# A Strassen-style FFN decoder trunk on one core: the fourth lead unit gets its own PSUM pair, and the products, cuts and sums around it are reordered

## The reference

```
x += 0.5 * SwiGLU_1(rms(x))                  # FFN, hidden width 2816
x += W_out [ gMLP(rms(x)) ; RG-LRU(rms(x)) ]
x += 0.5 * SwiGLU_2(rms(x))                  # FFN
x += sigmoid(rms(x) @ W_pg) * (p[i] @ W_pp)
# swiglu(x) = (silu(x @ wg) * (x @ wu)) @ wd
```

## Time and profile before

| | us |
|---|---|
| median of 3 runs | 1858.75 (1858.49 to 1860.04) |
| the profiled execution | 1858.88 |
| its span, first to last instruction | 1857.2 |
| TensorE busy | 1819.7 |
| VectorE busy | 1508.2 |
| ScalarE busy | 1063.0 |

### The profile page before, as it was taken

How to read it: one execution, slowest core, us unless ns; L and a number is a source line. 1 busy time by engine, 2 the same in 40 slices (tenths; PEclk the granted TensorE clock), 3 DMA queues, 4 the chain that set the end, 5 groups by cost and what they waited for, 6 DMA issues and landing times.

```text
span 1857.2 us, 37525 instructions
## 1 busy us (share of the span) xinstructions
PE 1819.7 (98%) x14824; PEld 1797.5 (97%) x14824; DVE 1508.2 (81%) x2319; ACT 1063.0 (57%) x1538; POOL 299.4 (16%) x380
## 2 busy tenths in 40 slices
PE   7999999999999999999999999999999999999997
PEld 6999999998999999999999999999999999999997
DVE  7989978768689889787689789777775897988775
ACT  6656656545456566565466565554544665655553
POOL 0011011340120110112110110115202101011122
PEclk9999999999999999999999999999999999999998
DMA  5657579722346666795355765794223657667941
GB/s 173 155 151 188 136 199 246 216 80 69 110 134 155 175 166 152 194 262 172 124 148 127 197 167 158 209 249 147 71 92 114 162 137 194 158 160 230 237 140 47
DMA packets 81265, 297.16 MB, mean 160 GB/s; under 512 B 9344, under 2 KB 11680, under 8 KB 79312
## 3 DMA queue, kind: packets, MB, share of 16 engines
q1 hardware_dynamic: 52592, 184.87, 30.9%
q0 software_dynamic: 28512, 110.03, 27.8%
HBM read 267.00 MB, written 25.74 MB: 158 GB/s over the span
## 4 chain that ended last, share of the span: by engine, by line
PE 89%; DVE 7%; issue 2%; ACT 1%; DMA 0%; DVEq 0%; SPq 0%; ACTq 0%
PE main L764 24%; PE main L730 19%; PE main L769 12%; PE aux L764 9%; PE main L926 9%; PE aux L769 5%; PE aux L926 4%; PE aux L1028 2%; PE main L819 2%; PE aux L730 1%; PE aux L976 1%; DVE w_lo L1690 1%; PE main L1028 1%; PE aux L1048 0%; DVE tmp L1854 0%
## 5 line engine op out<-in xcount | busy, mean ns | idle before, releaser
L764 PE MATMUL main<-part_hi,w_hi 128*128 128x260 f32 x1296 | 328.5, 284 | 8.8 <-DVE tmp L1854 5.3
L764 PE MATMUL main<-part_lo,w_hi 128*128 128x260 f32 x1296 | 326.6, 283 | 0.0
L764 PEld LDWEIGHTS main<-part_hi,w_hi 128*128 128x128 f32 x1296 | 244.5, 189 | 11.6 <-DVE tmp L1854 7.7
L764 PEld LDWEIGHTS main<-part_lo,w_hi 128*128 128x128 f32 x1296 | 244.5, 189 | 0.0
L622 POOL DMA_DIRECT2D w_lo<-weights_dram x104 | 90.3, 868 | 851.1 <-ACT w_lo L1154 842.5
L769 PE MATMUL main<-part_hi,w_lo 128*128 128x260 f32 x1296 | 213.7, 282 | 0.2 <-DMA w_lo<-weights_dram 0.2
L1166 ACT ACTIVATE w_hi<-tau 128x1024 fp32r<-128x1024 f32 x104 | 109.9, 1057 | 177.0 <-PE main L769 152.4
L730 PE MATMUL main<-part_hi,w_hi 128*128 128x260 f32 x944 | 192.6, 285 | 2.0 <-DVE tmp L1738 2.0
L730 PE MATMUL main<-part_hi,w_lo 128*128 128x260 f32 x944 | 189.8, 283 | 0.0
L730 PE MATMUL main<-part_lo,w_hi 128*128 128x260 f32 x944 | 189.5, 282 | 0.0
L764 PE MATMUL main<-sig,w_hi 128*128 128x260 f32 x1280 | 181.6, 284 | 5.7 <-issue 5.7
(11 more groups left out here) (325 smaller groups left out, 4544.1 us busy)
## 6 DMA issues: line engine op xcount, KB each, us to landing
raw<-weights_dram SPq DMA_DIRECT2D x344, 512.0 KB, 3.8
w_lo<-weights_dram POOLq DMA_DIRECT2D x104, 512.0 KB, 6.4
d_part<-tmp POOLq DMA_DIRECT2D x64, 260.0 KB, 5.3
x<-d_part POOLq DMA_DIRECT2D x16, 1040.0 KB, 14.3
x_spill<-x POOLq DMA_DIRECT2D x6, 1040.0 KB, 4.9
x<-x_spill POOLq DMA_DIRECT2D x6, 1040.0 KB, 9.8
x<-x_in_dram SPq DMA_DIRECT2D x4, 520.0 KB, 6.7
x<-tmp POOLq DMA_DIRECT2D x4, 520.0 KB, 3.2
```

The costliest lines, as they stand in the source:

```text
L764: pe.matmul(ps, hi_w[:, w], xx(k), start=(start and k == 0 and b == 0), stop=False, skip_group_check=True)
```

## The change

It does five things, in each of the four FFNs.

1. The fourth lead unit (up 1) goes to `aux[1]` instead of a main pair. It waits for `std_s` instead of `evac`, and P1(0) and P1(1) wait for older evacuations.
2. In the first chunk P2(1) moves from behind P7(0) to ahead of P6(0).
3. On DVE, `tau3`, `tau4`, `hidden_out(1)` and `hidden_lo(0)` move behind `lo12` of the first tile. On ACT `copy_p1(0)` moves ahead of `hi34`, and `h_lead(1)` behind `copy_p5(0)`.
4. The copy of the two lead tiles of h into x (`copy_lead`) becomes two DMAs with a semaphore each.
5. The raw sums of h tiles 0 and 1 move from the stage with c22(3) to the stage with c22(1), and their low part comes together with that of tiles 2 and 3.

```diff
+FOURTHS = tuple(t + 1 for t in THIRDS)
...
-SUM_ORDER = ((1, 0, 2, 3), (0, 1, 2, 3))
...
+    if tiles == tiles_of(0) and t < 2 and name != "P4" and (t, name) != (1, "P7"):
+        return ({"P1": 1, "P2": 2, "P6": 5, "P5": 6, "P7": 7}, {"P1": 3, "P2": 4, "P6": 9, "P5": 10})[t][name]
...
-            return aux[0] if g in THIRDS else main[main_slot(g)]
+            return aux[0] if g in THIRDS else aux[1] if g in FOURTHS else main[main_slot(g)]
...
-            def copy_lead(f, G):
-                pool.wait_ge(evac, G)
+            def copy_lead(f, G, k):
+                pool.wait_ge(evac, G - 2 * (LEAD - 1 - k))
...
-                pool.dma_start(x[:, XT - 2:XT, :], tmp[:, 2:4, :]).then_inc(lead_copy, 16)
+                pool.dma_start(x[:, XT - LEAD + k, :], T(2 + k)).then_inc(lead_copy[k], 16)
... TensorE: the fourth lead unit, P1, the order, the down product
-                    pe.wait_ge(evac, G + 1)
+                    pe.wait_ge(std_s, stat + 1)
                     acc(bank(G + 3), 3, XT, x_hi, x_lo).then_inc(unit, 1)
...
-                            pe.wait_ge(evac, G - 2 * (1 - t))
+                            pe.wait_ge(evac, G - 3 + t)
...
-                        if t == 1:
+                        if c and t == 1:
                             pe.wait_ge(evac, G)
...
                     P1(1)
+                    if first:
+                        P2(1)
                     P6(0)
                     P5(0)
                     P7(0)
-                    P2(1)
+                    if c:
+                        P2(1)
                     P4(0)
...
-                            pe.wait_ge(std_s, stat + 1)
+                            pe.wait_ge(evac, G)
                         down_part(0, 0, whole - 1, True)
... ScalarE
-                        if first and t == 2:
+                        if first and t == 0:
                             sums_hi(l, f, c, 0)
...
                         hi12(n, S)
+                        copy_p1(0)
                         hi34(n, S)
...
-                        h_lead(l, G - 2 * LEAD, 1)
...
                     copy_p5(0)
+                    if first:
+                        h_lead(l, G - 2 * LEAD, 1)
                     hi12(n + 2, S + 1)
... VectorE, the lead of FFN 1 and 3 (the others likewise)
                             sigma_lo(stat, 3)
-                            ahead(1, S0, S)
-                            ahead(2, S0, S)
-                            hidden_lo(0)
-                            hidden_out(1)
+                            tau1(S0, S)
+                            tau2(S0, S)
...
-                        if first and t == 2:
+                        if first and t == 0:
                             sums_raw(f, c, 0)
                             sums_raw2(f, c, 0)
...
-                        if not last and t >= pairs and k % 2:
+                        if not last and t >= pairs and k % 2 and not (first and t == 1):
                             sums_lo(l, f, c, k // 2)
                         if first and t == 2:
                             sums_lo(l, f, c, 0)
+                            sums_lo(l, f, c, 1)
...
                     if first:
                         lo12(n, S)
+                        tau_sums(0, (tau3, tau4))
+                        hidden_out(1)
                         lo34(n, S)
-                        dve.wait_ge(hhi, h)
-                        hi_, lo_ = hparts(l)
-                        dve.tensor_tensor(lo_[:, LEAD - 1, :], T(3), hi_[:, LEAD - 1, :], ALU.subtract).then_inc(hlo, 1)
+                        hidden_lo(0)
                         lo_b(n, S)
```

More of the change, by code:

```diff
@@ L136, in first_tile @@
     return TILES * (2 * l + which)
-SUM_ORDER = ((1, 0, 2, 3), (0, 1, 2, 3))
 SUM_AT = ({3: 0, 1: 1, 2: 2, 4: 3}, {1: 0, 3: 1, 2: 2, 4: 3})
 def sums_of(f, c, i):
-    return KH * (DOWN_CHUNKS * f + c) + SUM_ORDER[c].index(i) + 1
+    return KH * (DOWN_CHUNKS * f + c) + i + 1
 def sums_in(f, c):
@@ L178, in main_slot @@
     layer, k = divmod(g, GROUPS)
-    return (g + layer + (k >= G_GT + V_AFTER) + sum(g > t for t in THIRDS)) % 2
+    return (g + layer + (k >= G_GT + V_AFTER) + sum(g > t for t in THIRDS + FOURTHS)) % 2
 def trunk(nc, weights, x_in, p_in, vecs_in, ln_in, bs_in, ws_in, bd_in, sc_in, sh_in,
@@ L309, in trunk @@
         sh_lo = sem("sh_lo")
-        lead_copy = sem("lead_copy")
+        lead_copy = [sem(f"lead_copy{k}") for k in range(LEAD)]
         d_second = sem("d_second")
@@ L667, in gates @@
                         if c == 0 and t == 1:
-                            copy_lead(f, G)
+                            for k in range(LEAD):
+                                copy_lead(f, G, k)
                         if c and t == 1:
@@ L1341, in ffn @@
                         hi34(n, S)
-                    copy_p1(0)
+                    if c:
+                        copy_p1(0)
                     copy_p1(1)
@@ L1603, in sums_raw @@
                 if early:
-                    dve.wait_ge(lead_copy, 16 * (f + 1))
+                    for k in range(LEAD):
+                        dve.wait_ge(lead_copy[k], 16 * (f + 1))
                 if f:
@@ L1713, in free @@
                 pending[b] = False
-            def ahead(j, n, T_):
-                if j == 1:
-                    tau1(n, T_)
-                    tau2(n, T_)
-                    tau3(n, T_)
-                if j == 2:
-                    tau4(n, T_)
-                if j == 3:
-                    lo34(n, T_)
             def ffn(l, which, u0, g0):
@@ L1739, in gate_out, with hidden_out @@
                                               ALU.mult).then_inc(evac, 1)
-                        def hidden_out(k):
+                        def hidden_out(k, n=n, G=G, fs=fs):
                             dve.wait_ge(unit, n + 2 * k + 2)
@@ L1745, in hidden_out, with hidden_lo @@
                                               ALU.mult).then_inc(evac, 1)
-                        def hidden_lo(k):
+                        def hidden_lo(k, h=h):
                             dve.wait_ge(hhi, h + k + 1)
@@ L1769, in ffn @@
                             sigma_lo(stat, 3)
-                            tau3(S0, S)
-                            tau4(S0, S)
-                            hidden_lo(0)
                         elif which:
@@ L1824, in c11 @@
                         elif first:
-                            dve.wait_ge(hlo, h)
                             dve.wait_ge(evac, G)
@@ L1851, in c22 @@
                         if first and t < LEAD:
-                            dve.wait_ge(lead_copy, 16 * (f + 1))
+                            dve.wait_ge(hlo, h - LEAD + t + 1)
+                            dve.wait_ge(lead_copy[t], 16 * (f + 1))
                         free(2 + (S + t) % 2)
@@ L1926, in ffn @@
                     lo12(n + 2, S + 1)
+                    if first:
+                        hidden_lo(1)
                     c11_r(0)
```

## The result

| | before | after |
|---|---|---|
| median, us | 1859.09 (1858.17 to 1860.04, 6 runs) | 1866.85 (1864.7 to 1868.7, 6 runs) |
| profiled execution, us | 1858.88 | 1868.59 |
| its span, us | 1857.2 | 1866.9 |

The changed kernel is slower: ratio 1.0042, 95% interval 1.0029 to 1.0055, +7.8 us by the medians. Forecast were +4.5 us and 1863.3; the time lies inside the range, near its upper end. The profiled execution of after is one of its slower ones, so in the traces there are 9.7 us to explain.

The account below looks back on a forecast made before the run. TensorE, busy 98% of the span, was taken to bound the kernel. Leads +2.2, clock +1.2 and +1.9, sums -0.8 made +4.5 us on 1858.75, so 1863.3; range 1857 to 1867.5.

Parts of the forecast that it names:

- as forecast: The main case for the whole kernel: slower by +3 to +6 us, chance 0.50.
- rival (c): The clock falls in FFN 1 and 3 too, or longer in FFN 0: +7.5 us, 1866, chance 0.14.
- What bounds, and P7(0): TensorE bounds; P7(0) waits for `copy_u2(0)` behind `gate(2)` and its load, starting 6.1 us behind `tau4`'s end, or later.
- Cost 0: The two smaller lead-copy DMAs, issued by POOL ahead of `gate(2)`'s low load, cost nothing.
- `tau4` moved: On DVE `tau4` ends later: +0.54 us in FFN 0 and 2, 4.2 us in FFN 1 and 3.
- Stands: TensorE stands 2.5 to 4 us before P7(0) in FFN 0 and 2, 1 to 1.6 in FFN 1 and 3.
- Leads at full clock: P4(0) starts shift by -0.9, +1.9, -1.1, +1.9 us in FFN 0 to 3, restarts +0.4: sum +2.2.
- Sums: Moving the sums of h on DVE shortens the stand before P4(4): -0.2 us in each of four, -0.8.
- The clock: Low clock behind the lead stands: +1.2 us in FFN 2, +1.9 in FFN 0, 0 in FFN 1 and 3.
- The sum: All terms for the whole kernel: +4.5 us, 1863.3 us, slower by 0.24%.
- Rival (d): Faster: the sums bring all they can (-0.3 us), and where `gate(2)` does not wait for its load -7.4, 1851; chance 0.14.

Follow-up runs that it names:

- Experiment 1: The changed kernel with `copy_u2(0)` and `copy_p5(0)` ahead of `gate(2)` on ACT in the first chunk: 1859.88 us.
- experiment 4: The changed kernel with the second copy of a lead tile issued behind the low load of the third tile instead of ahead of it: 1866.69 us.
- Experiment 5: The kernel before, with only the sums of h spread (part 5 of the change): 1858.32 us.
- experiment 11: The changed kernel once more, unaltered, a single execution: 1873.84 us.
- experiment 3: The changed kernel with `tau3` and `tau4` back ahead of `lo12` of the first tile on DVE: 1856.52 us.
- experiment 8: The changed kernel with `copy_u2(0)`, `copy_p5(0)` ahead of `gate(2)`, P2(1) back between P7(0) and P4(0), `tau3`, `tau4` ahead of `lo12`: 1853.84 us.

## Why the prediction was right, and where it was too small

The waits were forecast rightly, one by one; the time came out higher, and +7.8 us lies outside the forecast's own band for "as forecast" (+3 to +6). It is nearest to rival (c), +7.5, of which one half ("or longer in FFN 0") came true in the profiled execution, with a longer stretch in FFN 2 besides.

**What bounds, and P7(0).** Right. `gate(2)` was released by the DMA in all four leads, and P7(0) by `copy_u2(0)`. Experiment 1 takes only that dependence away, and the stands go. The chain from `tau4`'s end to P7(0) measured 6.5, 6.6, 6.4 and 6.3 us in FFN 0 to 3, where 6.1 was taken from the earlier trace rows. The load behind it took 3.7 to 4.05, where FFN 0 and 2 had 3.5 before. In experiment 4, without the second copy beside it, it took 0.5 and 0.25 less in FFN 0 and 2; why it took 4.05 in FFN 1 with the copy and without, and 4.5 in FFN 3 of the kernel before, stays open. "Cost 0" for the copies may so be off by a few tenths per FFN; the medians don't show it.

**`tau4` moved.** Right: in FFN 1 from the start of `hi12` to the end of `tau4` 3.53 us were forecast (550.31 to 553.84) and 3.52 measured (553.56 to 557.08).

**Stands.** Forecast 2.5 to 4 before P7(0) in FFN 0 and 2, and 1 to 1.6 in FFN 1 and 3: measured 4.2 and 3.6, 1.7 and 1.4; two of the four are just above what was said. P6(0) near 45.2: 45.53, of which 0.3 is the late start. 0.7 before P4(0): 0.82, 0.68, 0.72, 0.68. None before the fourth lead unit and P1(1): none.

**Leads at full clock.** Forecast -0.9, +1.9, -1.1, +1.9 and 0.4 for restarts, +2.2. Measured, without clock and start: -0.5, +2.6, -0.8, +2.2, so +3.5 with the restarts. The 1.3 is the longer chain.

**Sums.** Forecast -0.2 each, -0.8: measured -0.2 each; the stand before P4(4) is 1.05 in the rows in all four, where 1.1 to 1.2 was said and 1.36 was the old one in three. Experiment 5 shows it by itself.

**The clock is the step that was mis-sized.** It said: "Only the second counts: between nothing and twice 1.52, I take +1.9", and +1.2 in FFN 2. Measured in the profiled execution: FFN 0 lost 57.59 - 54.10 - 2.12 = 1.4 ahead of P4(0) and 2.2 behind it, 3.6 in all; FFN 2 0.2 and 2.8, 3.0 in all. That is 6.6 in place of 3.1. Some 0.5 of it is the price of restarts rather than clock, since the same two distances are 0.1 longer each in FFN 1 and 3, at full clock; the clock's own share is 6.1, still twice the forecast. The size of the loss was read from one old stretch (1.52 in FFN 2), as though a longer stand cost the same once, or twice at most. A longer stretch stood in the old trace: in FFN 0, behind stands of 3.16 and 3.22, the clock was at 0.50 from 42.0 to 52.2, and P1(1) (43.05 to 45.99) and P6(0) (49.21 to 51.95) took 1.5 and 1.3 us longer than 1.44. Windows of the kernel before:

```profile
50.00:52.00 2.00, 2.00 (x11) 2.00 (x11) 1.97 (x4) 1.58 (x2) 0.23 (x1) 0.50 0.19 20
52.00:54.00 2.00, 2.00 (x17) 2.00 (x17) 1.66 (x4) 0.97 (x3) 0.63 (x1) 0.94 0.82 250
```

Here the clock stayed low through P7(0), P4(0) and the products behind. The Trainium skill ("TensorE: Matmul & The Clock Gate", section Terms) prices it as throttled time times one minus the granted share. The trace agrees once the stand inside is taken out: from 54.1 to 62.4 less 0.7 is 7.6 us, half of it 3.8, against 3.4 to 3.6 measured. What was missing was the length of the low stretch, not its price.

**The sum.** 3.5 + 6.6 - 0.8 + 0.3 (the start) = 9.6, against 9.7 in the profiled execution. The median is at +7.8, because the profiled execution lies 1.7 above it. How many low stretches a median run has is not traced; experiments 4 and 11 show that their number differs from run to run, and that the other half of rival (c), low clock in FFN 1 too, is real in some runs. That the median fell inside the range at all leans on this: the single execution of experiment 11 (1873.8) did not.

**Rival (d)** did not come: `gate(2)` waited for its load in all four leads, and the sums gave 0.2 each. The order can still win. Against the kernel before, experiment 3 gained 2.9 us and experiment 8, with `copy_u2(0)` ahead of `gate(2)` as well, 5.2. Freeing the copy alone (experiment 1) gained nothing over the kernel before.

## What to carry to other kernels

When an instruction is moved back in an in-order queue, look for the DMA that it frees, and follow what stands behind that DMA's reader on its own engine: here a swap of two lines on DVE was worth 10 us through a load, two ACT cuts, a copy behind them and the low clock that the stands brought. Filling an early stand of TensorE gains nothing if the product after it has a fixed release time; first bring the release forward, then place the filler, and time the edits together, since each one's worth hangs on the others. Before you compare starts of two traces, find a row ahead of the edit and measure from it. Count a stand of several us twice, once as idle and once as the low clock behind it, and give that second part a wide range.
